# Forgetting-attention score chunks at an even rate, with two query blocks a turn ahead and half of the columns loaded first

## The reference

```
log_f = jax.nn.log_sigmoid(f_logit.astype(jnp.float32))
c = jnp.cumsum(log_f, axis=1)
...
s = jnp.einsum('bqhd,bkhd->bhqk', q_i, k).astype(jnp.float32) * scale
s = s + c_i[..., None] - c_keys[:, :, None, :]
s = jnp.where(k_pos[None, :] <= q_pos[:, None], s, NEG)
p = jax.nn.softmax(s, axis=-1).astype(v.dtype)
return jnp.einsum('bhqk,bkhd->bqhd', p, v)
```

## Time and profile before

| | us |
|---|---|
| median of three runs (2583.35 to 2587.63) | 2583.76 |
| profiled execution, device time | 2577.67 |
| its span, first to last instruction | 2576.0 |
| PE busy in it | 2377.0 (92%) |
| DVE busy | 1371.8 (53%) |
| ACT busy | 1159.0 (45%) |
| one loop turn of `attend`, from one wait at step 26 to the next (677.79 to 745.49) | 67.7 |

### The profile page before, as it was taken

The page is one execution under the profiler, slowest core; times in us unless marked ns, Lnnn a source line. Parts: engine busy times, 40 slices in busy tenths (PEclk is TensorE's granted clock), DMA queues, the critical chain, the costliest instruction groups (busy, mean ns, idle before and its releaser), DMA issues.

```text
span 2576.0 us, 34875 instructions
## 1 busy us (share of the span) xinstructions
PE 2377.0 (92%) x11432; PEld 1959.5 (76%) x11432; DVE 1371.8 (53%) x2345; ACT 1159.0 (45%) x2217; POOL 755.9 (29%) x623
## 2 busy tenths in 40 slices
PE   7999999499999999499789998999999899999978
PEld 6788888477777777387678886788888788888866
DVE  6311111377778878366554447644455675444464
ACT  6211111387788787222445555555562233233242
POOL 2000000011111111123456567666553422000571
PEclk9999999799999999799999999999999999999999
DMA  5333333655555552877454543464548765454573
GB/s 175 114 122 122 122 122 130 157 137 137 145 147 147 145 134 53 240 230 228 132 180 147 160 143 110 144 209 146 153 156 303 276 200 193 139 173 150 209 248 135
DMA packets 235994, 419.40 MB, mean 163 GB/s; under 512 B 56008, under 2 KB 117064, under 8 KB 230088
## 3 DMA queue, kind: packets, MB, share of 16 engines
q1 hardware_dynamic: 229712, 400.97, 49.3%
q0 software_dynamic: 6144, 16.79, 2.7%
HBM read 281.03 MB, written 136.64 MB: 162 GB/s over the span
## 4 chain that ended last, share of the span: by engine, by line
PE 41%; DVE 4%; POOL 3%; DMA 1%; issue 1%; ACT 0%; SPq 0%; ACTq 0%; DVEq 0%
PE f_ps L1956 22%; PE f_ps L1977 20%; POOL h_raw L1673 2%; DVE f_hop_lo L1859 2%; POOL f_b_late L1673 1%; DVE f_op_lo L1848 1%; DMA f_b_late<-in_w_down 1%; DVE f_acc L1890 0%; DMA h_raw<-in_w_down 0%; DVE f_u L1878 0%; DVE hop_lo L1864 0%; DVE f_hop_lo L1870 0%; DVE f_op_lo L1851 0%; ACT f_hop_hi L1757 0%; DMA out<-wu_raw 0%
## 5 line engine op out<-in xcount | busy, mean ns | idle before, releaser
L1956 PE MATMUL f_ps<-f_hop_hi,f_op_hi 128*128 128x512 f32 x768 | 304.6, 397 | 25.8 <-DVE f_u L1878 14.6
L1956 PE MATMUL f_ps<-f_hop_hi,f_op_lo 128*128 128x512 f32 x768 | 303.4, 395 | 0.0
L1956 PE MATMUL f_ps<-f_hop_lo,f_op_hi 128*128 128x512 f32 x768 | 303.3, 395 | 0.0
L693 POOL DMA_DIRECT2D o_main<-a_o x64 | 37.8, 590 | 898.1 <-issue 471.7
L1848 DVE TENSOR_TENSOR f_op_lo<-wu_raw,f_op_hi 128x512 fp32r<-128x512 f32 x160 | 163.9, 1027 | 220.6 <-ACT f_op_hi L1724 220.6
L1851 DVE TENSOR_TENSOR f_op_lo<-h_raw,f_op_hi 128x512 fp32r<-128x512 f32 x224 | 189.1, 846 | 165.8 <-ACT f_op_hi L1728 165.7
L1977 PE MATMUL f_ps<-f_hop_hi,f_op_hi 128*128 128x512 f32 x672 | 263.2, 392 | 12.8 <-DVE f_op_lo L1851 12.8
L1977 PE MATMUL f_ps<-f_hop_hi,f_op_lo 128*128 128x512 f32 x672 | 262.2, 390 | 0.0
L1977 PE MATMUL f_ps<-f_hop_lo,f_op_hi 128*128 128x512 f32 x672 | 262.1, 390 | 0.0
L909 DVE TENSOR_TENSOR a_pt_lo<-a_ps_t,a_pt_hi 128x512 fp32r<-128x512 f32 (+1 forms) x352 | 213.0, 611 | 51.6 <-ACT a_pt_hi L1003 51.0
L360 PE MATMUL p_ps_o<-p_ht_hi,p_w_hi 128*128 128x512 f32 x608 | 237.2, 390 | 3.0 <-DVE p_w_lo L277 3.0
(11 more groups left out here) (174 smaller groups left out, 5435.9 us busy)
## 6 DMA issues: line engine op xcount, KB each, us to landing
h_raw<-u_ops SPq DMA_DIRECT2D x224, 256.0 KB, 3.8
wu_raw<-in_w_up SPq DMA_DIRECT2D x32, 1024.0 KB, 7.1
u_ops<-f_u SPq DMA_DIRECT2D x128, 256.0 KB, 4.1
u_ops<-f_us SPq DMA_DIRECT2D x96, 256.0 KB, 2.0
proj_hi<-p_o_hi SPq DMA_DIRECT2D x18, 1024.0 KB, 4.0
proj_lo<-p_o_lo SPq DMA_DIRECT2D x18, 1024.0 KB, 6.7
h_raw<-in_w_down SPq DMA_DIRECT2D x32, 512.0 KB, 4.1
h_raw<-in_w_down SPq DMA_DIRECT2D x49, 256.0 KB, 4.1
```

What stands on the lines that cost most here:

```text
L1956: last = nc.tensor.matmul(bank[:], w[:, k], h[i][:, k], start=(UP_OPENS[i] and k == 0 and m == 0), stop=(k == 3 and m == 2), skip_group_ch ...
```

## The change

The table `chunk_at` is filled otherwise. Block 2's chunks stand at steps 0 to 8, block 3's at steps 9 to 21, the next turn's swa chunks at steps 23 to 27, and then the chunks of both block 0 and block 1 of the next turn, twelve, one in each of the steps 30 to 41. The number of chunks per turn is the same. The prelude computes block 1 of turn 0 as well, and turn 7 has no chunks of block 0 and 1 left. `load_fox` cuts at 1024 columns rather than 512, so that `first` and `fox` are 2 MB each, and the wait for `fox` moves to chunk (2, 0, 0).

```diff
-    for b, (start, span) in ((1, (0, 5)), (2, (5, 7)), (3, (12, 12))):
-        for n, c in enumerate(fox_chunks[b]):
-            chunk_at[start + n * span // len(fox_chunks[b])].append(c)
-    for n, c in enumerate(swa_chunks):
-        chunk_at[26 + n * 6 // len(swa_chunks)].append(("next",) + c)
-    for n, c in enumerate(fox_chunks[0]):
-        chunk_at[36 + n * 6 // len(fox_chunks[0])].append(("next",) + c)
+    ahead = fox_chunks[0] + fox_chunks[1]
+    for chunks, start, span in ((fox_chunks[2], 0, 9), (fox_chunks[3], 9, 13)):
+        for n, c in enumerate(chunks):
+            chunk_at[start + n * span // len(chunks)].append(c)
+    for chunks, start, span in ((swa_chunks, 23, 6), (ahead, 30, 13)):
+        for n, c in enumerate(chunks):
+            chunk_at[start + n * span // len(chunks)].append(("next",) + c)
...
-                for cols, done in ((slice(0, BANK), qk_loaded["first"]), (slice(BANK, S), qk_loaded["fox"])):
+                for cols, done in ((slice(0, 2 * BANK), qk_loaded["first"]), (slice(2 * BANK, S), qk_loaded["fox"])):
...
-                    if (b, t, n) == (1, 0, 0):
+                    if (b, t, n) == (2, 0, 0):
                         pe.wait_ge(qk_loaded["fox"], QK_FOX * (head + 1))
...
-                    if (b, t, n) == (1, 0, 0):
+                    if (b, t, n) == (2, 0, 0):
                         dve.wait_ge(qk_loaded["fox"], QK_FOX * (head + 1))
                     if (t, n) == (0, 0) and h is not BEFORE:
-                        if b == 0:
-                            dve.wait_ge(turned, turn_count(h, ("p", BLOCK0[1] - 1)))
+                        if c[0] == "next":
+                            dve.wait_ge(turned, turn_count(h, ("p", BLOCK0[b + 1] - 1)))
```

## The result

The changed kernel takes 2544.6 us (median of 4 runs, 2541.1 to 2544.7) where the kernel before takes 2583.6: a ratio of 0.984, with a 95% interval of 0.9825 to 0.9859. The profiled execution took 2541.1 us with a span of 2539.4, 36.6 less than the span of before (2576.0, at a mean granted clock of 0.979 against 0.977 here). The forecast was 27 us less, 2557; the gain is 39 by the medians and 41 by the ratio, inside the range (a gain of 11 to 43). It lies in the case "better (over 34)", to which the prediction gave a chance of 0.08.

What follows compares the result with a forecast made beforehand. PE bounds the kernel, with gaps. Seven loop turns at 2.8 us give 20, turn 7 gives 7, the prelude nothing: 27 us off the median of 2583.8, 2557; range 2541 (gain 43) to 2573 (gain 11).

Steps and rivals of the forecast that it cites:

- better (over 34): Rival, whole kernel: all gaps but the start of the turn go, gain 46 us, 2538; chance 0.08 for gains over 34.
- Steps 6, 14, 26 and 25: Loop turn: PE's waits for exponentials and step 25's gap go, as chunks come earlier; 3.3 us gained.
- T: Moment in a loop turn when DVE has read chunk (3, 3, 3); with the change PE then begins step 23, not 25.
- Steps 31 to 34: Loop turn: PE's gaps go because chunks in steps 30 to 41 cover the path from transpose to `weigh`; 2.4 us gained.
- ACT's backlog at steps 28, 29 and 31: Loop turn: ACT's backlog of swa exponentials is moved, not dissolved, and still holds PE; 1.85 us stay.
- The wait for `first`: Loop turn, step 30: the 2 MB load lands 0.9 us later than PE asks, absorbing step 31's 0.35; costs 0.6 us.
- The start of a turn: DVE's 2.6 us idle at its jump back stays, now with two 512-wide chunks before its first subtraction; 0.2 us lost.
- Small gaps: Elsewhere in a loop turn: allowance for small gaps between full queues, 0.25 us lost.
- Turn 7: Last turn: loses eight chunks and its waits, with no load or swa work in the way; 7 of 7.4 us gained.
- The prelude: Before turn 0: the eight added chunks hide behind PE's wait for V and cost nothing; bounds -1 to +3 us.
- `first` lands in time: Rival, loop turns: the load arrives by T + 10.8, so no loss; 4 or 5 us more gain, 2552; chance 0.2.
- Slower: Rival, step 30: PE stands for `first`, landing at T + 16.3 or later; time 2590, chance 0.04.

Runs made afterwards that it cites:

- experiment 12: Changed kernel with blocks 2 and 3 ending as late as before (steps 0 to 11, 12 to 23), swa from 24, next blocks from 31: 2553.9 us, ratio 0.9877.
- experiment 7: Kernel before with only the next block 0's four chunks moved, to steps 30, 33, 36 and 39: 2583.9 us, ratio 0.9991.
- experiments 8 and 9: Changed kernel, swa chunks thinner, next blocks from step 31: (8) swa at 23, 24, 26, 27, 29, 2536.1 us; (9) every second step 22 to 30, 2534.4 us.
- experiment 10: Changed kernel with the load in three groups (columns 0 to 511, 512 to 1023, the rest), each with its own semaphore: 2542.0 us, ratio 0.9837.
- experiment 6: Changed kernel with 232 one-column writes on DVE ahead of attention, its loop 256 instructions behind the place in the kernel before: 2561.8 us, ratio 0.9906.
- experiment 1: Kernel before with only the changed load (2 MB `first`, `fox` awaited at chunk (2, 0, 0)), old chunk table: 2584.3 us, ratio 0.999.
- experiment 2: Changed kernel with the load of the kernel before (`first` 512 columns, `fox` awaited at chunk (1, 0, 0)): 2599.6 us, ratio 1.0044.

## Why the prediction was right in its range and short in its number

The loop turn was to gain 2.8 us, and a quiet one gains 4.85 (67.7 to 62.87). I read the gaps of PE in both traces from start to start, less the distance that two such starts usually have; the turn of before that begins at 743.52 has 8.3 us of gaps, that of after at 723.35 has 3.5.

- **Steps 6, 14, 26 and 25.** Forecast 3.3, measured 1.01 + 0.66 + 1.19 + 0.45 = 3.3, all gone. Part of the reason is refuted by experiment 12: it isn't the lead of two or three steps that removes the waits at 14 and 26, for they stay away without it. At step 14 it is the thinner rate. At step 26 it is the swa chunks behind block 3, since block 3's own steps are those of before, and in turn 7, which has no swa chunks, the wait stays at 1.1 us. The lead has another worth: T comes two steps earlier, and the load with it.
- **Steps 31 to 34.** Forecast 2.4, measured 2.6 (the smaller gaps counted). The reason, that PE's own work covers the path there, fails in experiment 7 (one chunk between them, at step 33, and the gaps of steps 32 and 34 are 0.85 and 0.79). What is left is that the swa exponentials moved ahead, out of these steps, with ACT's backlog.
- **ACT's backlog at steps 28, 29 and 31.** Forecast 1.85, measured 0.64 + 1.01 + 0.35 = 2.0. Its cause is shown by experiments 8 and 9, which thin it and take 0.57 us and some 1 us off a turn.
- **The wait for `first`.** Forecast 0.6 in each turn. Counted from the first issue, which the prediction puts at T + 0.3, it had `first` at 11.4 and PE asking at 10.5. PE asks at 10.4 (experiment 10), and chunk (0, 0, 0) starts at 10.9, 11.7, 11.0, 10.4, 10.8, 10.6 and 10.8 us in turns 0 to 6. So `first` was a little late in all but turn 3, by half of what was forecast on the average, and half way to the bound of 10.3 that the mean pace of all 5 MB gave. Against the 62.84 to 62.88 us of a turn with three groups this costs nothing in turns 3 to 5, where the gap of step 31 absorbs it, as the prediction had said, 0.1 us in turns 0 and 2, and 2.4 in turn 1: 0.4 a turn on the average of turns 0 to 5. Nearly all of it is what I left out, the clock, which fell once behind this wait.
- **The start of a turn.** Forecast 0.2 lost, since the 2.6 us at DVE's jump "stays". This step failed. It went, for a reason outside the order of work: eight chunks more ahead of the loop moved its code by 24 instructions. The start of a turn had 2.2 us of gaps and has 1.5, 0.5 of it the new wait for `a_o`: 0.7 gained, 0.9 a turn better than forecast. The price that I gave it had it stayed was wrong too, and more so: experiment 6 is 17 us slower than the changed kernel, 2.9 at each of six jumps, which less the 0.7 gained makes not 0.2 but some 2 us a turn lost. A small part of the gaps of before was something else: in its turns 1, 2 and 7 PE waits 0.96, 0.73 and 0.44 us for V, and after the change it doesn't.
- **Small gaps.** Forecast 0.25 lost, measured 0.17 gained.
- **Turn 7.** Forecast 7, measured 4.7. The step that failed is "no load and no swa work stand in its way": swa chunks are also cover, and without them ACT's exponential of 2.0 us stands ahead of a copy that PE needs two steps on. That is 1.2 us with the drain; a wait of 0.47 for `a_o` and one of 0.21 for `a_pt_lo`, also new, bring it to some 2 of the 2.3 missing. ACT and PE, steps 22 to 25:

```profile
974.50 2.00 ACT L980 ACTIVATE a_probs<-a_probs,a_nm_fox 128x2048 f32<-128x2048 f32 x1
```

```profile
976.33 0.27 PE L800 MATMUL a_ps_t<-a_ident,a_probs 128*128 128x128 f32 x1
977.62 0.44 PE L826 MATMUL a_ps_o<-a_pt_hi,a_v_fox 128*128 128x384 f32 x1 [1.01 <-DVE a_pt_lo L909]
```

- **The prelude.** Forecast 0 within -1 to +3, measured 2.6 gained, and by experiment 1 it is the load's. I had looked at what the chunks add and not at V, which stands last in the same queue: seven transfers of twice the size bring all of it 2.6 us sooner. Why they do wasn't tested.

So in size the errors of the loop come from the load term and the start of a turn, and outside it 2.3 us too much for turn 7 and 2.6 too little for the prelude nearly cancel, which is luck. With the idle at the jump in both kernels the change gains 24 us (experiment 6), with it in neither, 0.984 over 0.9972 or some 34 us; of the 41 us by the ratio some 7 belong to the place of the loop and not to the order of work. The forecast of 27 assumed the first of these worlds. That it comes near the 24 there is luck too: it priced the idle at 0.2 us a turn instead of 2, and had the gains of the rest too low.

The rivals: "`first` lands in time" describes the cost in turns 3 to 5, though only in turn 3 it was there when asked for. "Better than forecast" (2538) has the number more nearly than the forecast, but not its mechanism: 3.5 us of gaps stay in a turn, 2.0 of them ACT's backlog, and the one gap that it let stay is the one that went. "Slower" has the right mechanism, a stand at the load with the clock behind it, and experiment 2 shows what it costs when the load comes late enough; here it came in time.

## What to carry to other kernels

A table that asks for data earlier and the load that brings it are one change: price both, and each alone, since here one alone is worth some 3 us, the other costs 11, and both give 39. Before you call a gap at a loop's jump a fixed cost, look at the instruction queue's packets and count the loop's instructions, for any edit that adds code ahead of a loop can remove or bring such a gap, and its price depends on what stands first behind the jump. When PE waits for a copy, see what ACT has ahead of it: here more work on PE did not shorten a wait that ACT's backlog set (experiment 7), and thinning the exponentials did (experiments 8 and 9).

## What was not expected of the hardware

- A DVE loop of some 308 instructions cost 2.6 us at its jump, or nothing, by a shift of 24 instructions; some 30 packets of 8 KB (0.24 MB in 30) on the instruction queue tell which. Where the edges of the blocks lie was not measured.
- Behind waits of PE of 0.76, 0.99 and 1.09 us the granted clock fell, behind others of 0.85, 1.05 and 1.30 (experiment 9) it didn't, and a turn with a fall was some 2 us longer. Behind the six waits of 2.56 to 2.86 us in experiment 6 it fell five times, and behind 4.6 us and more in experiment 2 each time.
- The same 5 MB in the same number of transfers landed 2.6 us sooner when the first seven carried twice as much. No run shows why.
